# An eleventh early gate projection inside the latent stage of a two-block transformer kernel

## The reference, cut to what matters

```python
proj = h @ w_in
dq, dk, dv, iq, ik, iw, cq, ckv, kpe, gd, gm = jnp.split(proj, IN_OFFSETS, axis=-1)
...
q_b = (rms_norm(cq, mla_cq_g) @ mla_w_uq).reshape(b, s, MLA_HEADS, MLA_QK)
kv_b = (rms_norm(ckv, mla_ckv_g) @ mla_w_ukv).reshape(b, s, MLA_HEADS, MLA_NOPE + MLA_V)
k_nope, v_b = kv_b[..., :MLA_NOPE], kv_b[..., MLA_NOPE:]
k_pe = jnp.broadcast_to(kpe[:, :, None, :], (b, s, MLA_HEADS, MLA_ROPE))
k_b = jnp.concatenate([k_nope, k_pe], axis=-1)
...
merged = jax.nn.sigmoid(gd) * (out_a @ w_br_dsa) + jax.nn.sigmoid(gm) * (out_b @ w_br_mla)
return merged @ w_out
```

## Time and profile before

| what | before |
|---|---|
| median of three runs | 2367.02 us |
| lowest, highest | 2362.29, 2367.72 us |
| the profiled execution's own time | 2364.26 us |
| span of its profile | 2362.3 us |
| mean granted TensorE clock | 0.966 |
| PE busy | 2202.8 us (93%) |
| DVE, ACT, POOL busy | 1243.9, 1118.1, 730.5 us |
| DMA read and written | 247.98 and 14.18 MB |

### The profile page before, as it was taken

How to read it: one execution, slowest core, us unless ns; L and a number is a source line. 1 busy time by engine, 2 the same in 40 slices (tenths; PEclk the granted TensorE clock), 3 DMA queues, 4 the chain that set the end, 5 groups by cost and what they waited for, 6 DMA issues and landing times.

```text
span 2362.3 us, 29885 instructions
## 1 busy us (share of the span) xinstructions
PE 2202.8 (93%) x10776; PEld 1782.2 (75%) x10776; DVE 1243.9 (53%) x2212; ACT 1118.1 (47%) x1964; POOL 730.5 (31%) x479
## 2 busy tenths in 40 slices
PE   8999999989999999988988999998988888999997
PEld 6666777767888887766767888887867767788886
DVE  6766575558999634555555232224567355333233
ACT  6455554467888535545343332223776344332222
POOL 5261233410000222411333333224833424333233
PEclk9989999999999999989989999999999989999999
DMA  4402233218999530220212332331311221232331
GB/s 165 150 25 68 72 102 108 72 72 314 392 385 392 182 106 28 67 77 19 93 42 66 97 101 93 98 98 63 100 53 36 72 72 54 90 102 95 99 98 54
DMA packets 74529, 264.10 MB, mean 112 GB/s; under 512 B 8272, under 2 KB 8400, under 8 KB 74000
## 3 DMA queue, kind: packets, MB, share of 16 engines
q1 hardware_dynamic: 66816, 238.76, 29.3%
q0 software_dynamic: 2816, 11.82, 1.4%
q10 hardware_dynamic: 4752, 11.61, 1.3%
HBM read 247.98 MB, written 14.18 MB: 111 GB/s over the span
## 4 chain that ended last, share of the span: by engine, by line
PE 81%; DVE 7%; ACT 6%; issue 3%; POOL 2%; DMA 1%; POOLq 0%; DVEq 0%; ACTq 0%; SPq 0%
PE ps L511 17%; PE ps L513 16%; PE ps L512 16%; PE ps L1140 3%; PE ps L571 2%; PE ps L2851 2%; PE ps L2853 2%; PE ps L2852 2%; PE ps L1155 2%; PE ps L1174 2%; PE ps L547 2%; PE ps L548 2%; PE ps L553 2%; PE ps L2878 1%; PE ps L2879 1%
## 5 line engine op out<-in xcount | busy, mean ns | idle before, releaser
L453 ACT ACTIVATE wh<-raw 128x1024 fp32r<-128x1024 f32 x308 | 322.3, 1054 | 438.3 <-PE ps L513 408.3
L458 DVE TENSOR_TENSOR wl<-raw,wh 128x1024 fp32r<-128x1024 f32 x176 | 241.8, 1380 | 506.5 <-ACT wh L453 499.6
L511 PE MATMUL ps<-hh,wh 128*128 128x512 f32 (+1 forms) x1192 | 468.7, 393 | 6.2 <-POOL wl L458 5.9
L458 POOL TENSOR_TENSOR wl<-raw,wh 128x1024 fp32r<-128x1024 f32 x132 | 319.0, 2417 | 483.2 <-ACT wh L453 472.6
L512 PE MATMUL ps<-hl,wh 128*128 128x512 f32 (+1 forms) x1192 | 465.0, 390 | 0.0
L513 PE MATMUL ps<-hh,wl 128*128 128x512 f32 (+1 forms) x1192 | 464.9, 390 | 0.0
L511 PE MATMUL ps<-act,wh 128*128 128x512 f32 (+1 forms) x688 | 269.4, 392 | 14.2 <-ACT act L1415 9.9
L512 PE MATMUL ps<-act,wh 128*128 128x512 f32 (+1 forms) x688 | 267.4, 389 | 0.0
L513 PE MATMUL ps<-act,wl 128*128 128x512 f32 (+1 forms) x688 | 267.3, 388 | 0.0
L511 PEld LDWEIGHTS ps<-hh,wh 128*128 128x128 f32 (+1 forms) x1192 | 224.1, 188 | 55.7 <-issue 8.9
L513 PEld LDWEIGHTS ps<-hh,wl 128*128 128x128 f32 (+1 forms) x1192 | 223.9, 188 | 47.7 <-issue 0.4
(11 more groups left out here) (468 smaller groups left out, 3904.0 us busy)
## 6 DMA issues: line engine op xcount, KB each, us to landing
raw<-d_w SPq DMA_DIRECT2D x277, 512.0 KB, 3.7
raw_x<-d_moe SPq DMA_DIRECT2D x84, 512.0 KB, 6.5
raw<-d_moe SPq DMA_DIRECT2D x84, 512.0 KB, 6.6
d_xs<-Sb POOLq DMA_DIRECT2D x7, 514.0 KB, 8.7
Xb<-d_xs ACTq DMA_DIRECT2D x6, 514.0 KB, 5.7
area<-d_mem POOLq DMA_DIRECT2D x3, 1024.0 KB, 5.6
d_ys<-rows ACTq DMA_DIRECT2D x6, 512.0 KB, 5.6
xT<-d_x SPq DMA_DIRECT2D x8, 256.0 KB, 6.2
```

The costliest lines, as they stand in the source:

```text
L453: me.e.activation(hi, raw, ACT.Copy).then_inc(*me.done("wh", m))
L458: me.e.tensor_tensor(lo, raw, hi.bitcast(F32), ALU.subtract).then_inc(*me.done("wl", m))
L511: me.e.matmul(bank[0:m, 0:n], wh[:, c], hi, start=k == 0, stop=False)
```

## The change

Gate 7 becomes an early gate. Its product stands in the latent stage, behind the four `kn` products and before the common key's turning product. Its tile is in `pool_blocks`, its kept copy goes into `S[:, 1, 3, :]`, a score tile that is not used at that time, and from there it is stored like the others, behind ACT's part of the latent stage. The first exponentials of the attention wait for that store. ACT, DVE and POOL each get a call `ahead(("gate", 7))`: ACT's stands behind its eight `kn` copies and before the squares of `qr`, DVE's and POOL's are the first thing in their part of the stage. In the last stage gate 7 is left out and loaded back from DRAM.

```diff
 def latent_pe(K, me):
     for c in range(4):
         linear(K, me, ("L", "kn", c), "mla_w_ukv", 0, K.c_kn[c], K.src_kv, 128, after=[("raw", "kn", c)])
+    gate_pe(K, me, K.g_rot)
     bank = K.banks[me.take("ps", "rot", "mlar", 0)]
...
@@ latent_act, behind the loop over kn
+    ahead(K, me, ("gate", K.g_rot))
     for r in range(2):
         me.wait_ge("L", "qr", r)
         square_of(K, me, ("qr", r), K.bank("L", "qr", r), ("ss", "qr", r))
+    gate_kept_act(K, me, K.g_rot)
     heads_root_act(K, me, "mlak")
...
 def latent_dve(K, me):
+    ahead(K, me, ("gate", K.g_rot))
...
 def latent_pool(K, me):
+    ahead(K, me, ("gate", K.g_rot))
     xn = K.tdn("xh", "mlar", 0)[COMMON, :]
...
-    K.early_gates = (2, 3, 5, 6, 8, 9, 11, 12, 14, 15)
+    K.early_gates = (2, 3, 5, 6, 7, 8, 9, 11, 12, 14, 15)
+    K.g_rot = 7
...
-    for m in (6, 8, 9, 11, 12):
+    for m in (6, 7, 8, 9, 11, 12):
...
-    K.gate_home = {2: a[:, 16, :], 3: a[:, 17, :], 5: a[:, 18, :], 14: a[:, 0, :], 15: a[:, 1, :]}
-    K.gate_war = {2: [], 3: [], 5: [], 14: [("end", "pe", "mla_att")], 15: [("end", "pe", "mla_att")]}
+    K.gate_home = {2: a[:, 16, :], 3: a[:, 17, :], 5: a[:, 18, :], 7: K.S[:, 1, 3, :], 14: a[:, 0, :], 15: a[:, 1, :]}
+    K.gate_war = {2: [], 3: [], 5: [], 7: [], 14: [("end", "pe", "mla_att")], 15: [("end", "pe", "mla_att")]}
...
     latent_act(K, me)
+    gate_spilled_act(K, me, K.g_rot)
     values_act(K, me, "vb", K.i_vb)
...
-    attention_act(K, me, "mla_att", K.i_mla_att, first=[("keys", 7), ("tok", "mlar", 2), ("zeros", NBLK - 1)], pt_first=[("sine", 2, 1)], ticks=1)
+    attention_act(K, me, "mla_att", K.i_mla_att, first=[("keys", 7), ("tok", "mlar", 2), ("zeros", NBLK - 1), ("spilled", 7)], pt_first=[("sine", 2, 1)], ticks=1)
```

More of the change, by code:

```diff
@@ L2038, in mixer_dve @@
     values_dve(K, me, "vb", K.i_vb)
-    attention_dve(K, me, "mla_att", K.i_mla_att, first=[("keys", 7), ("tok", "mlar", 2), ("zeros", NBLK - 1)], pt_first=[("sine", 2, 1)], ticks=2)
+    attention_dve(K, me, "mla_att", K.i_mla_att, first=[("keys", 7), ("tok", "mlar", 2), ("zeros", NBLK - 1), ("spilled", 7)], pt_first=[("sine", 2, 1)], ticks=2)
     ahead(K, me, ("gate", 11))
```

## The result

The changed kernel takes 2376.01 us (median of ten, 2368.86 to 2377.69) against 2362.64 us (median of ten, 2355.94 to 2368.75) for the kernel before: ratio 1.0046, 95% interval 1.0033 to 1.0059. It is slower. The forecast was 2376 us with a chance of 0.65 for slower, from a sum of +9.1 us; the ratio says +10.9 us (0.0046 of 2362.64). The two medians by themselves are 13.4 us apart, a quotient of 1.0057. The recorded ratio is not that quotient, and both lie in the interval.

What follows compares the result with a forecast made beforehand. PE, busy for 93% of the span, was taken as the bound. The terms -5.4 + 4.6 + 7.3 + 1.7 + 0.9 = +9.1 us on 2367.02 gave 2376 us, range 2362 to 2388.

Steps and rivals of the forecast that it cites:

- term 2: Latent stage: POOL's early splits delay its key sums and PE's second query turning; +4.6 us, bounds 3.6 to 11.
- term 4: Start of the last stage: gate 1's second half moves from DVE to POOL and PE waits; +0.9 us.
- term 3: Key head after the attention: low half moves to DVE behind the masks; PE waits +7.3 us, low clock adds +1.7.
- Term 1: Last stage: gate 7's 24 matmuls leave a stage where PE never waits; -5.4 us.
- The sign that I gave for it: Profile sign for the product's removal: a last stage of 68.8 us in place of 74.2.
- Both waits hidden: Rival: early splits on ACT and POOL bring the query turning 3 to 6 us sooner; 2358 us, chance 0.10.
- One wait only: Rival: the key head's half is ready in time, leaving +0.1 us; 2367 us, no change, chance 0.14.
- The low clock to the end: Rival: key spreads and `qn` from 164.8 stay at 1.2 GHz; latent cost 11, sum +15.5, 2383 us, chance 0.14.

Runs made afterwards that it cites:

- again: The changed kernel unedited, measured a second time on another chip against the kernel before: 2373.22 us, ratio 1.0038.
- the fourth experiment: The kernel before, without gate 7's change, with only the key head's low half moved from POOL to DVE: 2370.42 us, ratio 1.0033 against the kernel before.
- the one with both edits: Changed kernel with the key head's low half back on POOL and without POOL's early ahead call: 2356.63 us, ratio 0.9977 against the kernel before.
- the kernel with the old engines: Changed kernel without POOL's early ahead call, tiles from gate 6 to 35 split by their former engines: 2353.45 us, ratio 0.9957 against the kernel before.
- the first experiment: Changed kernel with the key head's tile entered in pool_blocks, so POOL writes its low half: 2368.36 us, ratio 1.0029 against the kernel before.
- The kernel with only the other wait: Changed kernel without POOL's ahead call at the head of its latent stage: 2364.14 us, ratio 1.0001 against the kernel before.

## Why the prediction was right

**Direction and size.** +9.1 us was forecast; the ratios give +10.9 (7.8 to 13.9) and, again, +9.0. That the forecast of 2376 us meets the median of 2376.01 is luck: it was built on a median of 2367.02 of three runs, and that kernel's ten runs have 2362.64, from which the same sum gives 2371.7. The sum is close in part because its errors have both signs: term 2 and term 4 and the stage left out came dearer, term 3 cheaper.

**Term 1, -5.4:** measured -5.45 by making the product again. The sign that I gave for it, 68.8 us in place of 74.2, was for the stretch that ends at 392.00; the whole last stage went from 81.20 to 77.15, terms 1 and 4 together.

**Term 2, +4.6:** measured +6.1. The steps held one by one: POOL's splits at 147.3 (forecast 148.0), key sums ending at 163.2 (163.8), the second query turning at 164.14 (164.75), DVE's first key at 168.68 (168.9), and the variance 14.27 us behind it (14.07).

But this execution began the stage 0.74 us earlier. Counted from the first `kn` product, the first key came 5.2 us later than before where the working gives 4.6, because the key spread before it ran at low clock too (1.92 us for 1.05); the chain behind it took 0.2 longer, and the end 0.8. I let ACT's saved split (1.0 us) pull PE's first `vb` turn forward and let PE's own work take that back. Measured from DVE's variance to the first score product it is 6.7 us (182.95 to 189.65) against 5.9 before (178.33 to 184.25): the saved split was eaten by a fall of the clock. By the trace it came about so: PE, once the clock was back at 171, ran through `qn` and `vb` faster than DVE's chain and then waited 2.84 us for ACT, longer than the 1.27 before. The stretch from there to the first score product was 4.15 us for 2.76.

This fall does not belong to the change alone: in the fourth experiment, with the stage of before, it came as well (a wait of 4.62 us, then 5.00 us to the first score product). Against that execution the changed kernel's stage is 3.3 us longer, not 6.1. So +4.6 lies between the two readings, and neither decides it to better than 3 us; the wait of 7.50 us and what removed it are certain. The bounds were 3.6 to 11.

The granted clock did not fall at 139, and `qr` took 3.70 us for 6.56. The Trainium skill, TensorE: Matmul & The Clock Gate, What's actually happening, says that the clock is throttled by default and that activity releases it. The trace agrees at this place. It shows falls as well where PE's records have no idle time (about 150.8 in the changed kernel, 149.5 in the one with both edits), and why they come there is open.

**Term 3, +7.3 and +1.7:** measured +5.8 and +1.5 in the changed kernel. The tile numbers, DVE's missing call and its first one behind the masks were right. The mis-sized piece is the masks: I took their 2.47 us from the trace of before, where POOL was splitting `dv` beside them, and I had moved that very split to DVE two paragraphs earlier. The fourth experiment, where POOL keeps `dv`, shows 7.3 us between the spread and the key head beyond the usual 0.4: the forecast figure, but for a kernel that is not the changed one.

**Term 4, +0.9:** measured 1.9, by the kernel with the old engines: a wait of 0.8 us as forecast, 0.5 more in the wait behind the stage, and 0.6 of slower matmuls in between, which I had put at nothing.

**Left out:** the sparse attention, +1.6 in both profiles of the changed kernel. It is not there with the key head back on POOL (46.85) or without POOL's early call (46.74). By the trace PE reached `dv`'s turn early, waited 1.62 us for ACT and made the first score products at low clock (4.12 us for 2.43). The wait alone does not do it: in the fourth experiment PE waited 1.64 us at the same place and these products took 2.43. I put it at nothing; what makes the clock low there was not tested and stays open.

**The rivals.** Both waits hidden: excluded by the two waits, but the kernel it describes exists, and runs at 0.9957, as the 2358 (0.996 of 2367) that I gave it. One wait only, with the key head's half in time: that is the kernel of the first experiment, and it ran at 1.0029 (1.0016 to 1.0043) where I gave it no change. The kernel with only the other wait ran at 1.0001. The low clock to the end: it was low for 7 us behind the second turning (about 164 to 171.3) and again around `vb`'s turns (185.5 to 188.4), not for all 26.

## What to carry to other kernels

Where engines run hand-ordered lists, price an added step by what it makes each of them stand for: here one call placed first in POOL's list, waiting for ACT, cost more (7.35 us of the stage) than the 24 matmuls that it served (5.45). When work is inserted into a numbered plan, list what changes hands behind it; a rule like "odd tiles on POOL" turns one insertion into many reassignments, and one of these cost 0.3%. And when two changes touch the same moment, take each duration from the state after both: a row of before may carry a collision that the change itself removes. Before a stage's length in one profile is set against another's, look for a second execution of the same code: here two of them differ by 2.9 us, half of what was to be explained.

## What the runs showed of the hardware that I had not expected

- DVE's one-input mask instructions take 2.4 us in place of 0.89 for three when POOL's split runs beside them (254.46 to 256.8 in the fourth experiment); one of them took 1.82 us where its like takes 0.35. The same collision decides what DVE's gained copy of the common part takes at 139 to 140.5: in all the profiles it is 0.48 us while POOL's addition beside it takes 1.56 to 1.59, or 1.58 to 1.62 while POOL's takes 1.26 to 1.29. Which engine loses differs between executions of one kernel (0.48 and 1.62 in the changed one). In the kernel before PE stood 3.92 us behind the short copy and 5.02 behind the long one; with gate 7 in the gap it stands for neither.
- The granted clock falls while PE is busy without a gap, in the sums of squares with 128x2 products or in the products just behind them, and whether it falls there differs from one execution to the next: `qn`'s eight instructions took 3.68, 5.38, 5.99 and 6.28 us in four kernels with the same code there, and 5.38 and 3.68 in two executions of the changed kernel.
- A PE that is made faster inside a stage whose end another engine sets waits longer, and may lose its clock in that wait: 2.84 us in front of `vb`'s turn in the changed kernel, 4.62 in the fourth experiment, and the turns at 1.2 GHz behind both; behind 1.27 us in the first profile they ran at 2.4 GHz.
